# A decoder layer's expert stage: a quarter of each V row's sum moved from TensorE to VectorE

## The reference, cut to what matters

```python
def chunk(xc):                                  # 128 tokens at a time
    ...
    expert = ia * PEER_KEYS + ib                # 8 heads x 16 picks = 128 experts for each token
    g = jax.nn.softmax(best_s, axis=-1)
    u = u_tab[expert]
    a = jax.nn.gelu(jnp.einsum('cd,chkd->chk', xc, u), approximate=False)
    coeff = g * a
    return jnp.einsum('chk,chkd->cd', coeff, v_tab[expert])
out = rms_norm(h + that)
```

## Time and profile before

| | us |
|---|---|
| median of 3 runs | 4094.79 |
| lowest and highest of them | 4079.92, 4095.18 |
| the profiled execution | 4086.41 |
| its span, first to last instruction | 4084.6 |

### The profile page before, as it was taken

How to read it: one execution, slowest core, us unless ns; L and a number is a source line. 1 busy time by engine, 2 the same in 40 slices (tenths; PEclk the granted TensorE clock), 3 DMA queues, 4 the chain that set the end, 5 groups by cost and what they waited for, 6 DMA issues and landing times. The chain is left out here.

```text
span 4084.6 us, 33485 instructions
## 1 busy us (share of the span) xinstructions
PE 3284.0 (80%) x9134; PEld 1561.4 (38%) x9134; DVE 2166.0 (53%) x4954; ACT 1300.4 (32%) x3397; POOL 1374.5 (34%) x1367
## 2 busy tenths in 40 slices
PE   8689888758784878887869689779878977987776
PEld 6544445323232444544433234234323423432222
DVE  0311112166847667766615745854774585477444
ACT  1011113211221434433323433443443344344333
POOL 0000000024533767766612233333333332333332
PEclk9889997879897899999989899999999999999999
DMA  7610112499997999998978799999999999999998
GB/s 290 226 55 23 32 51 103 141 330 384 333 326 265 363 343 368 355 376 306 361 315 300 294 372 394 420 370 379 415 383 368 405 417 359 376 416 412 422 420 354
DMA packets 283743, 1288.75 MB, mean 316 GB/s; under 512 B 27440, under 2 KB 52144, under 8 KB 193072
## 3 DMA queue, kind: packets, MB, share of 16 engines
q0 software_dynamic: 195120, 1073.83, 67.5%
q1 hardware_dynamic: 83696, 195.62, 13.1%
q10 hardware_dynamic: 4752, 17.30, 1.2%
HBM read 1243.65 MB, written 42.99 MB: 315 GB/s over the span
## 5 line engine op out<-in xcount | busy, mean ns | idle before, releaser
L454 PE MATMUL e_acc<-s_ring,s_diagonal 128*128 128x512 f32 x2296 | 1149.1, 629 | 353.0 <-ACT s_diagonal L310 307.4
L380 DVE CUSTOM_DVE_ANT_0 s_ring<-s_ring,e_x_copy 128x1024 f32<-128x1024 f32 x581 | 704.9, 1217 | 460.3 <-DMA s_ring<-peer_uv,s_expert 399.5
L454 PEld LDWEIGHTS e_acc<-s_ring,s_diagonal 128*128 128x128 f32 x2296 | 427.8, 197 | 1026.9 <-ACT s_diagonal L310 549.4
L264 POOL DMA_INDIRECT s_ring<-peer_uv,s_expert x462 | 435.9, 943 | 868.0 <-PE e_acc L454 687.4
L454 PE MATMUL e_acc<-e_more_slots,s_diagonal 128*128 128x512 f32 x948 | 469.8, 622 | 108.1 <-ACT s_diagonal L310 98.7
L310 ACT ACTIVATE s_diagonal<-s_ident,s_gate 128x128 f32<-128x128 f32 x1024 | 396.8, 398 | 333.3 <-PE e_acc L454 221.1
L264 POOL DMA_INDIRECT s_ring<-peer_u,s_expert x331 | 358.1, 1082 | 398.8 <-DVE s_expert L1637 232.7
L264 POOL DMA_INDIRECT s_ring<-peer_v,s_expert x325 | 347.5, 1069 | 346.9 <-PE e_acc L454 123.3
L327 ACT ACTIVATE s_dots<-s_dots 128x1 f32<-128x1 f32 x704 | 141.5, 201 | 943.2 <-DVE s_dots L380 941.9
L380 DVE CUSTOM_DVE_ANT_0 e_more_slots<-e_more_slots,e_x_copy 128x1024 f32<-128x1024 f32 x231 | 281.0, 1218 | 209.7 <-DMA e_more_slots<-peer_uv,s_expert 207.3
L264 POOL DMA_INDIRECT e_more_slots<-peer_uv,s_expert x231 | 218.4, 945 | 435.5 <-PE e_acc L454 329.1
(11 more groups left out here) (206 smaller groups left out, 3423.9 us busy)
## 6 DMA issues: line engine op xcount, KB each, us to landing
e_halves<-peer_scores SPq DMA_DIRECT2D x12, 2048.0 KB, 16.1
e_halves<-mem_scores SPq DMA_DIRECT2D x6, 2048.0 KB, 14.7
e_halves<-mem_values SPq DMA_DIRECT2D x6, 2048.0 KB, 19.7
p_w_in<-w_in SPq DMA_DIRECT2D x8, 1104.0 KB, 15.4
f_w_big<-w_mem_kv SPq DMA_DIRECT2D x4, 2048.0 KB, 15.7
f_w_big<-peer_w_q_t SPq DMA_DIRECT2D x2, 4096.0 KB, 17.8
peer_scores<-f_stage_s SPq DMA_DIRECT2D x16, 512.0 KB, 3.6
s_ring<-peer_uv,s_expert POOLq DMA_INDIRECT x462, 8.8
```

Of the source, the lines that this page charges most:

```text
L264: pool.indirect_dma_start(out=to, out_offset=None, in_=table, in_offset=bass.IndirectOffsetOnAxis(ap=self.expert[c % PICK_BUFFERS][:, k:k ...
L380: dve.tensor_tensor_reduce(row, row, x[:, :], 1.0, 0.0, ALU.mult, ALU.add, self.dots[:, k:k + 1]).then_inc(self.u_used, 1)
L454: last = pe.matmul(self.acc[:, at:at + BANK], self.diagonal[:, made % DIAGONALS, :], row[:, at:at + BANK], start=(n == group[0]), stop=(n ...
```

## The change

In the last stage TensorE multiplies and adds only the first 768 columns of each V row: a block of 512 and one of 256. VectorE adds up the last 256 columns in a buffer of its own, `e_part` (128 x 256), in SBUF. It does so one pick behind: at the position of the V row of pick g, behind the dot product of pick g, it adds the row of pick g-1. It waits there for the row, for the coefficient of that pick (`coeff_made`) and for its own last add. The first add of each chunk is a plain multiply that overwrites the buffer. For the picks before position 662 the add is of the same pick. GpSimd waits in addition for VectorE's add (`v_dve`) before it fetches into a slot that held a V row of the last stage. At the end of a chunk `end_sum` makes two adds, 768 columns of `acc` and 256 of the buffer, and `end_root` and TensorE's next chunk wait for both. The first two stages are as before.

```diff
+        self.columns = [columns for _, _, columns in stages]
-            dve += kind == "v" and self.stages[s][2] == "split"
+            dve += kind == "v" and self.columns[s] < D
     def pe_columns(self, n):
-        return D if self.mode(n) == "pe" else BANK
+        return self.columns[self.stage_of[n]]
...
                     pool.wait_ge(self.v_pe, self.pe_through[m])
-                    if self.mode(m) == "split":
+                    if self.pe_columns(m) < D:
                         pool.wait_ge(self.v_dve, self.dve_through[m])
...
+            elif self.pe_columns(n) < D:
+                if n < PAIRS_AT:
+                    self.add_part(n)
+                elif n - 2 >= PAIRS_AT:
+                    self.add_part(n - 2)
+                if n == len(ROWS) - 1:
+                    self.add_part(n)
+    def add_part(self, n):
+        dve = self.nc.vector
+        g = ROWS[n][1]
+        rest = slice(self.pe_columns(n), D)
+        row, part = self.row(n)[:, rest], self.part[:, :]
+        self.wait_row(dve, n)
+        if g >= ALONE_FROM:
+            dve.wait_ge(self.coeff_made, g - ALONE_FROM + 1)
+        else:
+            dve.wait_ge(self.coeff_ready, g // TOPK + 1)
+        if n == self.group(g // PICKS, self.stage_of[n])[0]:
+            dve.tensor_scalar(part, row, self.coeff(g), None, ALU.mult).then_inc(self.v_dve, 1)
+        else:
+            dve.wait_ge(self.v_dve, self.dve_through[n] - 1)
+            dve.scalar_tensor_tensor(part, row, self.coeff(g), part, ALU.mult, ALU.add).then_inc(self.v_dve, 1)
...
+        if self.mode(last) == "pe" and columns.stop < D:
+            rest = slice(columns.stop, D)
+            dve.tensor_tensor(self.h[:, rest], self.part[:, :], self.h[:, rest], ALU.add).then_inc(self.h3_ready, 1)
+        dve.wait_ge(self.h3_ready, self.summed(c))
...
             for at in range(0, self.pe_columns(n), BANK):
-                last = pe.matmul(self.acc[:, at:at + BANK], self.diagonal[:, made % DIAGONALS, :], row[:, at:at + BANK],
+                to = min(at + BANK, self.pe_columns(n))
+                last = pe.matmul(self.acc[:, at:to], self.diagonal[:, made % DIAGONALS, :], row[:, at:to],
                                  start=(n == group[0]), stop=(n == group[-1]))
...
-STAGES = [(PICK_02, "pe"), (ATTEND_37, "split"), (len(ROWS), "pe")]
+STAGES = [(PICK_02, "pe", D), (ATTEND_37, "split", BANK), (len(ROWS), "pe", 3 * D // 4)]
```

More of the change, by code:

```diff
@@ L121, in __init__ @@
         self.nc, self.io = nc, io
-        self.stages = [(start, until, mode) for start, (until, mode) in zip([0] + [u for u, _ in stages], stages)]
+        self.stages = [(start, until, mode) for start, (until, mode, _) in zip([0] + [u for u, _, _ in stages], stages)]
+        self.columns = [columns for _, _, columns in stages]
+        assert all(mode == "split" or columns == D or s == len(stages) - 1 for s, (_, mode, columns) in enumerate(stages))
         self.ident = sb("s_ident", [P, P])
@@ L137, in __init__ @@
         self.x_copy = None
+        self.part = None
         self.row_loaded = [sem(f"s_row_loaded{i}") for i in range(WIDE_RING)]
@@ L211, in pe_columns, with summed @@
     def pe_columns(self, n):
-        return D if self.mode(n) == "pe" else BANK
+        return self.columns[self.stage_of[n]]
+    def summed(self, c):
+        return sum(1 + (self.mode(CHUNK_END[d]) == "pe" and self.pe_columns(CHUNK_END[d]) < D) for d in range(c + 1))
     def row(self, n):
@@ L385, in vector @@
                 self.wait_h(c, self.dve_through[n] - 1)
-                half = slice(BANK, D)
-                dve.scalar_tensor_tensor(self.h[:, half], row[:, half], self.coeff(g), self.h[:, half], ALU.mult,
+                rest = slice(self.pe_columns(n), D)
+                dve.scalar_tensor_tensor(self.h[:, rest], row[:, rest], self.coeff(g), self.h[:, rest], ALU.mult,
                                          ALU.add).then_inc(self.v_dve, 1)
-        self.at["vector"] = max(until, self.at["vector"])
+            elif self.pe_columns(n) < D:
[5 more added lines that the diff above has]
+                    self.add_part(n)
+        self.at["vector"] = max(until, self.at["vector"])
+    def add_part(self, n):
+        dve = self.nc.vector
+        g = ROWS[n][1]
+        rest = slice(self.pe_columns(n), D)
+        row, part = self.row(n)[:, rest], self.part[:, :]
[9 more added lines that the diff above has]
+            dve.scalar_tensor_tensor(part, row, self.coeff(g), part, ALU.mult, ALU.add).then_inc(self.v_dve, 1)
     def picks_free(self, c):
@@ L1386, in pick_chunks @@
         stream.x_copy = ps("e_x_copy", [P, D])
+        if resident and stream.columns[-1] < D:
+            stream.part = sb("e_part", [P, D - stream.columns[-1]])
         block = ctx.enter_context(nc.Block())
```

5 lines of the change are left out of this document (2 added, 3 removed).

## The result

| | before | changed |
|---|---|---|
| median, us (6 runs each) | 4087.45 | 4057.63 |
| lowest and highest | 4079.74, 4095.18 | 4041.49, 4065.28 |
| ratio | | 0.9924, 95% interval 0.9908 to 0.9940 |
| profiled execution: time, span | 4086.41, 4084.6 | 4065.17, 4063.4 |

The change makes the kernel 0.8% faster, about 30 us, clear of the 0.5% bound. The forecast was 4090, no change. The whole range holds the result, A's own range (4074 to 4115) does not, and rival B (4052) is the nearest case. The likeliest case was not the one that came.

What follows compares the result with a forecast made beforehand. The DMA's ceiling was taken to bound the late phases and the picks alone, TensorE the early phases. TensorE's gain of 67 and VectorE's loss of 62 gave -5 us from 4094.8, so 4090; whole range 4045 to 4132.

Steps and rivals of the forecast that it cites:

- A: The forecast itself: TensorE's gain and VectorE's loss nearly cancel, 4090 us, own range 4074 to 4115; chance 0.43.
- rival B: Faster: early phases come close to the DMA's ceiling and VectorE's waits are fully used, 4052 us; chance 0.28.
- The gapless row: Early stretch 3170 to 3233: TensorE busy 63.00 of 63 us, taken to show that TensorE sets the pace there.
- the 44% of weight loads: Skill's rule, same stretch: weight loads measure TensorE's load; at 44% it would seem free and the change bring no gain.
- D: Slower: serial chains, not matmuls, set the early phases, so TensorE's faster blocks bring nothing, 4157 us; chance 0.04.
- TensorE's gain: Early phases: TensorE's shorter picks let the DMA set the pace; 4 x 15 plus 7 in the first, 67 us.
- I take 15: Gain in us for each full early phase, between 5 and 16.5, since short stalls pass under the pairs in flight.
- VectorE's loss: Late phases: adds of 0.49 us exceed VectorE's waits for rows; 4 x 12 plus 14 in the first, 62 us.
- The slot's release: Ring: a slot comes free at 3280.74 against 3280.79 before, so GpSimd's new wait costs nothing where the DMA sets the pace.
- Rival C: Slower: late slots come free later, gathers start later and VectorE waits for rows again, 4122 to 4154 us; chance 0.25.
- E: Picks alone: TensorE, less busy, may get a lower clock; 12 us at the very most, no case of its own.
- if the late phases keep 150 us: Sign that the forecast is wrong; it expected late phases of about 161 us and early ones of about 190.

Runs made afterwards that it cites:

- e1: Against the kernel before, TensorE adds only 768 of 1024 columns in the last stage and nobody adds the other 256: ratio 0.9879, 4041.9 us against 4091.4.
- second profile: The changed kernel itself, run again on another chip: ratio 0.9936 to the kernel before, 4074.2 us against 4103.1.
- e5: Against the kernel before, TensorE adds only 512 of 1024 columns in the last stage and VectorE none: ratio 0.9777, 4016.5 us against 4108.9.
- e2: Against the kernel before, TensorE keeps all 1024 columns and VectorE also adds the last 256 into a buffer nobody reads: ratio 1.0058, 4115.7 us.
- e3: Against the changed kernel, VectorE's adds read its own buffer instead of the V row, so GpSimd need not wait for them: ratio 0.9903 to the kernel before.
- e4: Against the changed kernel, VectorE adds two picks behind instead of one: 4132.8 us, ratio 1.0100 to the kernel before.
- e9: Against the changed kernel, VectorE adds the same pick's row directly behind its dot product, and end_sum comes one position earlier: ratio 1.0096 to the kernel before.

## Why the prediction was right or wrong

**What bounds the kernel: right.** Three kinds of phase, one ceiling. The changed kernel still has 326 us for the picks alone, and no variant has moved that below 323.9. Nearly all of the gain came where the DMA was below its ceiling: e1 gains 49 us in the opening and the early phases and 6 in the late ones. The first late phase lies below it as well (321 GB/s), but there VectorE, busy 90.5 of 100 us, holds it back, and e1 gains nothing. The gapless row was the right guide and the 44% of weight loads was not: e1 only takes columns off TensorE and gains 50 us.

**TensorE's price: right.** 1.29 us for a pick (3052.31 - 3051.02). D, that TensorE's columns bring nothing, is refuted by e1.

**TensorE's gain: right in kind, too large.** 67 us expected, 45 measured; e1, without the adds, has 50 in all. The failing term is "I take 15": the four full early phases gave 9.2, 4.3, 10.7 and 5.8, a mean of 7.5 (8.2 in the second profile, 8.7 in e1), nearer to the lower end of 5. The step behind it is that a stall "passes under" the six pairs. From 3025 to 3221 the stalls still cost: against one pick in 2.49 us the dot products fall back by 9.5 us over the first five picks and by 6 over the five from pick 675 on, 16 of the 21 us that the phase loses in all. TensorE's waits for ScalarE even grew, from 15.8 to 23.1 us. The reading above is that at 0.34 us a pick TensorE isn't always done with one stall when the next comes; e5 shows the room that was left. The first early phase went the other way, 14.9 instead of 7. The forecast counted the 23 picks there and left out the 22 V rows of the opening, and the two are one stretch: together they gave 13.9 us, and 13.8 in e1.

**VectorE's loss: right in kind, too large by far.** 62 us expected, 13 measured. The 13 are net of what TensorE's half gives in the late phases; the adds by themselves cost 19 to 20 there (against e1, and in e2), and 24 in all by e2's time. The failing term is the add's price of 0.49. Its length was right, as the instructions of line 421 show (ns: min, median, max):

```profile
L421 DVE SCALAR_TENSOR_TENSOR e_part<-s_ring,s_gate,e_part x474: 457/480/547, 2062.8 to 4049.8; 128x256 f32<-128x256 f32 x158
```

But what an instruction takes from its engine is not its length. Four instructions of VectorE in a late phase:

```profile
3250.18 1.22 DVE L388 CUSTOM_DVE_ANT_0 e_more_slots<-e_more_slots,e_x_copy 128x1024 f32<-128x1024 f32 x1
3251.32 0.09 DVE L388 DVE_READ_ACCUMULATOR2_ANT s_dots<- 128x1 f32 x1
3251.32 0.48 DVE L421 SCALAR_TENSOR_TENSOR e_part<-e_more_slots,s_gate,e_part 128x256 f32<-128x256 f32 x1
3251.71 0.68 DVE L1669 TENSOR_REDUCE e_place_f<-e_work 128x32 f32<-128x512 f32 x1
```

The add starts together with the read of the dot product's result, and the next instruction starts 0.39 us after it. That holds for 52 adds of this phase, at 0.38 to 0.40 us. Line 421 alone, and the waits for rows, in the late phase from 3221 to 3371:

```profile
3221.00:3371.00 150.00, 27.59 (x58) 0.94 1.00 409
```

```profile
DVE s_ring L388 <- DMA s_ring<-peer_uv,s_expert: 1.3, 2, 0.9
DVE e_more_slots L388 <- DMA e_more_slots<-peer_uv,s_expert: 1.0, 1, 1.0
```

VectorE's busy time went from 124.9 to 144.7 us, so 58 adds brought 19.8, or 0.34 each. Against them stand the waits for rows, down from 17.6 to 2.3, and the gaps between VectorE's own dependent steps: 149 - 124.9 - 17.6 = 6.6 us before, 150 - 144.7 - 2.3 = 3.0 now. The adds fill such gaps, which I had not counted as room. 15.3 and 3.6 together are 18.9 of 19.8, and the phase is 0.2 to 1 us longer than before, and 2 longer than in e1. In the first late phase the dot products had no wait to be used, and it lost 5.5 us, not 14: the busy time rose by 8.7 us and the idle time fell from 9.5 to 5.9.

By its table the Trainium skill, VectorE: DVE Perf Modes, section on the TRN2 errata, gave an estimate of 0.33 us for the add. The trace has 0.48 for its length and 0.34 for what it adds to busy time. The section gives its figure as the duration of a single instruction and says itself that it is too low for that, which agrees with the 0.48. That it comes near the 0.34 may be chance: no run here tells. The same page, section The DRAIN you can't avoid, says that an instruction that isn't held starts earlier than the pipeline's flush behind the one ahead, which agrees with the 0.39.

**The slot's release: right for one pick.** I reckoned the same moment. In the late phase GpSimd waits for slots as long as before (93 and 96 us), only now mostly for the adds (76) and hardly for TensorE. e3 puts the cost at 4 to 6 us by its profile and 9 to 14 by time, neither clear of noise. Rival C was real as a mechanism, with its point in another place: not reached with one pick behind, and worth 67 to 72 us with two (e4).

**The coefficient: not always in time.** The forecast took the wait for it as met in general. VectorE stands for it 41 us in 13 places of the changed kernel, mostly in the early phases. It had room there, and no run shows a cost.

**The clock.** 0.98 among the picks alone, and 0.80 to 0.96 in the phases where it had been 0.93 to 1.00. It fell, as E allowed, and among the picks alone it cost nothing that shows: 326.0 us against 324.9. In the other phases no run tells its cost apart.

**The sum.** -67 + 62 stood for -45 + 13 (and +1 for the rest) by phase, and for -50 + 24 by cause. Both terms were too large, by phase the loss by 49 and the gain by 22, and their balance, on which "no change" rested, was an accident of two estimates. Rival B's 4052 lies near for the same reason: it stood for a gain of 101 and a loss of 58. What was asked for as a sign of error ("if the late phases keep 150 us") is what happened, and the early phases ended at 196 to 203 us, not 190.

## What to carry to other kernels

Price an added instruction by the distance from start to start in a crowded stretch, and count as room both the engine's waits and the gaps between its dependent steps. An engine that must catch up after stalls can be worth speeding up even when its pace already lies below the bound; what counts then is the distance between the two. Before work is moved to an engine that frees buffers, count how many buffers each step behind holds: here one pick behind was right, and none (e9) and two (e4) both cost about 70 us against it. Move the work only in the phases where the receiver has room.

## What the runs showed of the hardware that was not expected

With TensorE on 512 columns its granted clock among the picks alone was 0.63, so most of the time 1.2 GHz, and the stretch took as long as before, 324 us (e5, by stretch):

```profile
3681.00:4005.00 324.00, 235.90 (x256) 57.51 (x255) 159.01 (x259) 119.61 (x390) 117.98 (x125) 0.63 1.00 417
```

Its matmuls fill 235.9 us of it, more than the 203.6 that the changed kernel needs there for half as much work again. A busy share without the clock beside it misleads: TensorE did less and looked busier.
